# Three modulation pairs moved from the state loop into the transposed projections

## The chip, the cores and the metric

The kernel runs on one core of one Trainium2 chip. The metric is the device time of one execution in microseconds; the median of three runs of the kernel before is 743.1 us. The engines are PE (TensorE), DVE (VectorE), ACT (ScalarE), POOL (GpSimd) and SP (SyncE, which here only issues DMAs). Each works through its own list of instructions in order and waits on semaphores.

## What is computed

One step of a one-layer hybrid encoder, for 512 prompt rows and 32 sample rows of width 1024, in fp32. Cut to what matters here:

```
sh1, sc1, gt1, sh2, sc2, gt2 = split(silu(c) @ ada_w + ada_b, 6)      # c: one row for the prompt, one for the sample
h = x * (1 + sc1) + sh1
gq, gk, gv, gr, ga, sq, sk, sv = split(h @ w_in)                       # one combined projection
loga = log_sigmoid(ga @ a2_w + a2_b) / 16
o_gla, state = chunkwise gated linear attention of gq, gk, gv, loga    # 4 heads, chunks of 64 rows
o_swa = windowed attention of sq, sk, sv                               # 8 heads, 2 of keys, window 128
mix = concat(rms_norm(o_gla) * silu(gr), o_swa) @ w_o
x = layer_norm(2**0.25 * x + gt1 * mix)
h2 = x * (1 + sc2) + sh2
x = layer_norm(2**0.25 * x + gt2 * mixture_of_experts(h2))             # 32 experts, the top 2 of a group
```

## The kernel before

Every engine has a list written out by hand; nothing reorders it. The stages follow one another in the profile like this.

**Modulation.** The 6144 columns of `ada_w` are cut into 12 pairs of 512 columns. A pair is two loads of 1 MB (units `("ada", 2p)` and `("ada", 2p+1)`, the two halves of the contracted 1024 rows) and, on PE, `ada(p, bk)` (L879 to L897): 4 small matmuls for the bias and 32 matmuls with two stationary columns (prompt and sample) over 128 weight columns each. DVE copies the result out with `mod_evac` (four copies into `modst`, which raise `ada_ev`). Pairs 0 to 3 are sh1 and sc1 and come first, since `h` needs them. Pairs 4 and 5 are gt1, 6 and 7 sh2, 8 and 9 sc2, 10 and 11 gt2; these are the later pairs, needed only after the output projection.

**Transposed projections.** PE computes ten blocks with `proj_t(tb, ...)` (L927 to L943): ga, gq (two blocks), gk (two), sq0 (two: tb 5 and 6), sq1 (two: tb 7 and 8) and sk (tb 9, from the unit `kv`). Each fp32 product is done as three passes over a high and a low part of both factors. For that ACT copies each 1 MB weight unit into a rounded high part (`high_unit(q)`, raises `iw_h`) and DVE subtracts it to leave the low part (`low_unit(q)`, raises `iw_l`); PE waits for `iw_l`. ACT also copies every finished block out of PSUM (`evac_t(tb)`, raises `t_ev`), and `proj_t(tb)` waits for the copy of block tb-2. The order on ACT is fixed (L695 to L707): ..., `evac_t(6)`, `high_unit(4)` (the unit kv), three exponentials of 128x1088 for the gates, `evac_t(7)`, `evac_t(8)`, `high_unit(5)` (the unit gv0), `evac_t(9)`.

**Row projections and window attention.** `proj_kv` makes sv, sk by rows in banks 3 and 4, then the wide projections gv and gr (units gv0, gv1, gr0, gr1) are woven into the window attention.

**State loop** (L1085 to L1109). For each of five row tiles: PE transposes the decayed keys into bank 0 (L1090), ACT copies them out (L765), PE multiplies them with the values (L1102, banks 6 and 7), DVE updates the carried state (L1539, four small operations, raises `u_ev`), and the next product waits for that. In the first three turns PE also computes pairs 4, 5 and 6 (`ADA_STATE`), with the copy-out on DVE ahead of that turn's state update.

**GLA output** computes scores and outputs, with pairs 7, 8 and 9 between (`ADA_GLA`), then the output projection, routing, and 36 expert turns that stream 3 MB of weights each.

**Weight loads.** SP issues them in the order of the list `units`: the eight ada units of pairs 0 to 3, the nine projection units gq, gk, sq0, sq1, kv, gv0, gv1, gr0, gr1, the twelve ada units of pairs 4 to 9, four units of `w_o`. They go into a ring of five 1 MB slots. Ahead of each load SP waits until the slot's former unit has been used:

```
if former(n) is not None:
    sp.wait_ge(*freed(former(n)))
```

A wait on SP holds up every load behind it. The slot of kv was last held by ada unit 7, so in this kernel its load is asked for once the fourth pair is done, ahead of the projections. After `gr1` the ada units of pair 4 wait for the units gv0 and gv1 to be used, the next three for the end of all row projections.

**Tiles.** `areaC` is a scratch area; its first 2560 columns hold the values `gv`, which DVE writes only during the window attention. `modst` is part of `modrt`, whose whole width also holds the attention scores of every other row tile (`Ssc[1]`).

Of the kernel before, what the change touches and what calls it, by code (L numbers as in the profile page):

```python
# [5 lines left out]
def hymba_stream_step(nc, x_prompt, x_sample, c_prompt, c_sample, state_gla, cache_swa_k, cache_swa_v,  # L6
# [71 lines left out]
    for u in range(NA1, NA2):  # L78
        units.append(("ada", u))
# [14 lines left out]
    with ctx:  # L94
# [101 lines left out]
        gt2_tiles = [[ring[:, NR - 1, :], gt2w], [ring[:, FREE, :], gt2w]]  # L196
        gt2st = areaC[0:98, 8 * D:8 * D + UC]
# [79 lines left out]
        h_high, h_low, ga_high = sem("h_high_parts"), sem("h_low_parts"), sem("ga_high")  # L277
        s_gtw = [sem("gt2_weights0"), sem("gt2_weights1")]
# [90 lines left out]
        ADA_STATE = {0: NPAIR1, 1: NPAIR1 + 1, 2: NPAIR1 + 2}  # L369
# [19 lines left out]
        FIRST = [(1, 2), (0, 2), (0, 0), (0, 1), (1, 0), (2, 0), (1, 1), (2, 1), (2, 2)]  # L389
# [4 lines left out]
        def _(sp):  # L394
# [3 lines left out]
            for n, (kind, u) in enumerate(units):  # L398
# [15 lines left out]
                if former(n) is not None:  # L414
                    sp.wait_ge(*freed(former(n)))
                for g, src in unit_src(kind, u):
                    if kind == "wo":
                        v = slot_view(n, 2)
                        dst = v if g is None else v[g * HD:(g + 1) * HD, :, :]
                    elif kind in ("ada", "gv0", "gv1", "gr0", "gr1"):  # L420
                        dst = slot_view(n, KD // 2)
                    elif kind in ("sq0", "sq1"):
                        dst = slot_view(n, KD)[:, :, g * HD:(g + 1) * HD]
                    else:
                        dst = slot_view(n, KD)
                    sp.dma_start(dst, src).then_inc(full[place(n)], 16)
# [58 lines left out]
        def _(pool):  # L485
# [44 lines left out]

            pool.wait_ge(tok_ev, NT)
# [24 lines left out]
            def store_mod(c, n, staged):  # L556
                for t in range(4):
                    dst = mod_d[:, c * D:(c + n) * D].rearrange("b (p t c) -> b p t c", t=4, c=P)[:, :, t, :]
                    pool.dma_start(dst, staged[32 * t:32 * t + 2, :].rearrange("b (p c) -> b p c", c=P)).then_inc(s_mod, 16)

            pool.wait_ge(ada_ev, NPAIR1 + 2)
            store_mod(2, 1, modst[:, 4 * P:6 * P])
# [3 lines left out]
            store_mod(3, 2, modst[:, 6 * P:10 * P])  # L566
# [12 lines left out]
            store_mod(5, 1, gt2st)  # L579
# [288 lines left out]
        def _(pe):  # L868
# [10 lines left out]
            def ada(p, bk):  # L879
                if p < NPAIR2:  # L880
# [10 lines left out]
                for k in range(KD):  # L891
                    if k == KD // 2 and p < NPAIR2:
                        wait_unit(ns[1])
# [76 lines left out]
            for q in (2, 3):  # L970
                pe.wait_ge(iw_l, q + 1)
                for b in range(2):
                    proj_t(tb, unit_parts(q), slice(b * P, (b + 1) * P)).then_inc(pe_t, 1)
                    tb += 1
            pe.wait_ge(iw_l, 5)
# [3 lines left out]
            pe.transpose(bank[1][:, 0:WIN], kc[:, :], ident[:, :]).then_inc(pe_t, 1)  # L979


            def proj_kv(m):
# [3 lines left out]
                if m >= 2:  # L986
                    pe.wait_ge(tok_ev, m - 1)
# [97 lines left out]
            for j in range(NT + 1):  # L1085
                if j < NT:
                    r = ROWS[j]
                    pe.wait_ge(kd_ev, j) if j >= 1 else pe.wait_ge(z_ev, 10)
# [17 lines left out]
                if j in ADA_STATE:  # L1106
                    p = ADA_STATE[j]
                    pe.wait_ge(tok_ev, len(TOK)) if j < 2 else pe.wait_ge(ada_ev, p - 1)
                    ada(p, 3 + p % 2)  # L1109
# [16 lines left out]
            def gla_out(j):  # L1126
# [5 lines left out]
                else:  # L1132
                    pe.wait_ge(ada_ev, NPAIR1 + 3)
# [219 lines left out]
        def _(dve):  # L1353
# [77 lines left out]
            low_unit(4)  # L1431

# [28 lines left out]

            low_unit(5)
            for m in range(NT):
# [9 lines left out]
            def scores(j, g):  # L1473
# [6 lines left out]
                for par in range(2):  # L1480
                    dve.wait_ge(pe_qk, 4 * j + 2 * g + par + 1)
                    h0 = 4 * par + 2 * g
# [43 lines left out]
            for j in range(NT):  # L1526
                if j in ADA_STATE:
                    mod_evac(ADA_STATE[j], 3 + ADA_STATE[j] % 2)
# [333 lines left out]
```

## Time and profile before

| | |
|---|---|
| median of 3 runs | 743.1 us (741.85 to 743.35) |
| the profiled execution | 743.77 us, of which 741.5 us from its first to its last instruction |
| busy in it | PE 617.3 us (83%), DVE 327.8 us, ACT 135.0 us, POOL 103.2 us |
| loads in the span | 181.03 MB, mean 244 GB/s |

All times of the trace are counted from the first instruction. The lead-in ends near 40 us, the transposed projections fill 40 to 114 us, the row projections and the window attention 114 to 225 us, the state loop 225 to 248 us, the GLA output 248 to 294 us, output projection and routing 294 to 407 us, the experts 408 to 700 us, and the last sums and norms the rest. Shares of busy time are averages over all of these.

### The profile page before, as it was taken

To read this page: it belongs to the slowest core of one execution; us is meant where nothing else is said; L and a number is where in the kernel's file an instruction comes from. 1 tells how busy PE (TensorE), PEld (TensorE's weight loads), DVE (VectorE), ACT (ScalarE), POOL (GpSimd) and SP (SyncE) were. 2 spreads that over 40 slices of the span, in tenths; PEclk is the share of its full clock that TensorE was granted. 3 is DMA by queue.
4 is the path that set the end of the run, shared out by engine and by line. 5 is a ranking of instruction groups with operands and counts; after the bars stand their busy time and mean duration, and the time that the engine had idled before them with its cause. 6 is when DMAs were issued, how large, how long until landed. Compare 5 with 4: busy or idle time off the path is not lost.

```text
span 741.5 us, 10794 instructions
## 1 busy us (share of the span) xinstructions
PE 617.3 (83%) x4458; PEld 392.8 (53%) x4458; DVE 327.8 (44%) x592; ACT 135.0 (18%) x356; POOL 103.2 (14%) x144
## 2 busy tenths in 40 slices
PE   3679999899998798999754999888888878878494
PEld 2459999676765564454443655444444444435241
DVE  2463361655524552375675245433333333343248
ACT  1442351334343053011120100000000000000100
POOL 3000000100001202000012233322222222222100
PEclk9979999999998587999955899988999999989797
DMA  8981330003009798501499599999999999996243
GB/s 301 369 220 58 66 114 2 14 1 114 1 3 383 257 384 213 197 29 42 170 364 356 196 408 408 408 405 407 406 408 408 408 400 398 402 399 267 77 187 117
DMA packets 75899, 181.03 MB, mean 244 GB/s; under 512 B 22164, under 2 KB 26108, under 8 KB 75844
## 3 DMA queue, kind: packets, MB, share of 16 engines
q1 hardware_dynamic: 65220, 163.39, 59.5%
q0 software_dynamic: 7936, 14.09, 5.5%
q10 hardware_dynamic: 2688, 2.77, 1.1%
q8 instruction: 40, 0.66, 0.4%
q14 instruction: 15, 0.12, 0.0%
HBM read 176.25 MB, written 14.45 MB: 257 GB/s over the span
## 4 chain that ended last, share of the span: by engine, by line
PE 48%; SPq 25%; DVE 11%; DMA 8%; issue 4%; ACT 3%; DVEq 0%; ACTq 0%; POOLq 0%
SPq L431 24%; PE bank L941 9%; PE bank L1175 7%; PE bank L1279 6%; PE bank L1008 6%; PE bank L1297 3%; DMA ring<-in_moe_w_up_dram 3%; DMA ring<-in_ada_w_dram 2%; PE bank L895 2%; PE bank L990 2%; DMA x_tok<-in_x_sample_dram 2%; PE bank L1138 1%; PE bank L1061 1%; PE bank L1142 1%; PE bank L1032 1%
## 5 line engine op out<-in xcount | busy, mean ns | idle before, releaser
L1279 PE MATMUL bank<-late_w,xT 128*64 128x256 f32 x672 | 88.5, 423 | 19.8 <-DMA late_w<-in_moe_w_up_dram 15.9
L1279 PEld LDWEIGHTS bank<-late_w,xT 128*64 128x64 f32 x672 | 55.1, 152 | 59.3 <-DMA late_w<-in_moe_w_up_dram 26.5
L1279 PE MATMUL bank<-ring,xT 128*64 128x256 f32 x480 | 65.6, 435 | 16.9 <-DMA ring<-in_moe_w_up_dram 15.1
L1759 DVE COPY xT<-bank 128x512 f32<-128x512 f32 x36 | 24.7, 692 | 124.1 <-PE bank L1265 123.7
L1279 PEld LDWEIGHTS bank<-ring,xT 128*64 128x64 f32 x480 | 39.6, 157 | 47.2 <-DMA ring<-in_moe_w_up_dram 23.9
L838 ACT ACTIVATE sgl<-bank 128x128 f32<-128x128 f32 x36 | 10.0, 278 | 250.0 <-PE bank L1279 250.0
L601 POOL DMA_INDIRECT expert_rows<-ye,dsti x36 | 36.6, 1016 | 125.1 <-DVE ye L1778 125.1
L594 POOL DMA_INDIRECT xg<-h_scratch,srci x38 | 38.9, 1025 | 105.7 <-PE bank L1265 94.1
L1775 DVE SCALAR_TENSOR_TENSOR S<-bank,modrt,S 128x512 f32<-128x512 f32 x36 | 27.0, 751 | 37.3 <-PE bank L1297 37.3
L1297 PE MATMUL bank<-late_w,hT 128*64 128x512 f32 x168 | 40.7, 604 | 1.2 <-issue 1.2
L1008 PE MATMUL bank<-ring_r,h_high 128*128 128x512 f32 (+1 forms) x140 | 38.4, 415 | 0.0
L895 PE MATMUL bank<-ring,csT 128*2 128x128 f32 x704 | 30.9, 342 | 4.5 <-DMA ring<-in_ada_w_dram 4.5
L941 PE MATMUL bank<-h_high,ring_r 128*128 128x272 f32 (+2 forms) x224 | 32.4, 293 | 0.0
L941 PEld LDWEIGHTS bank<-h_high,ring_r 128*128 128x128 f32 x224 | 29.9, 188 | 0.8
L1297 PE MATMUL bank<-ring,hT 128*64 128x512 f32 x120 | 29.1, 604 | 1.2 <-issue 1.2
L1008 PEld LDWEIGHTS bank<-ring_r,h_high 128*128 128x128 f32 (+1 forms) x140 | 23.8, 178 | 8.9 <-issue 1.8
L1175 PE MATMUL bank<-ring,areaA 128*128 128x512 f32 x64 | 28.5, 598 | 0.0
L1175 PE MATMUL bank<-ring,areaB 128*128 128x512 f32 x64 | 28.1, 592 | 0.0
L895 PEld LDWEIGHTS bank<-ring,csT 128*2 128x2 f32 x704 | 20.1, 102 | 14.4 <-DMA ring<-in_ada_w_dram 5.3
L1265 PE MATMUL bank<-ident,xg 128*128 128x128 f32 x144 | 23.8, 291 | 4.6 <-DMA xg<-h_scratch,srci 4.6
L1776 DVE SCALAR_TENSOR_TENSOR ye<-bank,modrt,S 128x512 f32<-128x512 f32 x36 | 26.7, 742 | 0.0
L1778 DVE TENSOR_TENSOR ye<-ye,S 128x512 f32<-128x512 f32 x36 | 24.9, 692 | 1.2
(309 smaller groups left out, 883.3 us busy)
## 6 DMA issues: line engine op xcount, KB each, us to landing
ring<-in_ada_w_dram SPq DMA_DIRECT2D x22, 1024.0 KB, 10.3
late_w<-in_moe_w_gate_dram SPq DMA_DIRECT2D x21, 1024.0 KB, 16.5
late_w<-in_moe_w_up_dram SPq DMA_DIRECT2D x21, 1024.0 KB, 20.1
late_w<-in_moe_w_down_dram SPq DMA_DIRECT2D x21, 1024.0 KB, 19.9
ring<-in_moe_w_down_dram SPq DMA_DIRECT2D x15, 1024.0 KB, 20.1
ring<-in_moe_w_gate_dram SPq DMA_DIRECT2D x15, 1024.0 KB, 16.4
ring<-in_moe_w_up_dram SPq DMA_DIRECT2D x15, 1024.0 KB, 20.2
ring<-in_w_in_dram SPq DMA_DIRECT2D x7, 1024.0 KB, 6.0
```

Source lines behind the costliest of these rows:

```text
L431: sp.dma_start(dst, expert_src(e, r)).then_inc(w_gu[k] if r < 2 else w_dn[k], 16)
L594: pool.indirect_dma_start(out=xg[:, a, :], out_offset=None, in_=h2_d[:, :], in_offset=bass.IndirectOffsetOnAxis(ap=srci[:, b:b + 1], axis= ...
L601: pool.indirect_dma_start(out=yb_d[:, :], out_offset=bass.IndirectOffsetOnAxis(ap=dsti[:, b:b + 1], axis=0), in_=ye[:, a, :], in_offset=No ...
L895: mm = pe.matmul(bank[bk][32 * t:32 * t + 2, 0:P], cs3[:, :, k], w[2 * k // KD][:, k % (KD // 2), t * P:(t + 1) * P], start=False, stop=(k ...
L941: mm = pe.matmul(bank[bk + tb % 2][0:m, 0:ts.stop - ts.start], w[pw][:, k, cs], hHL[ph][:, k, ts], start=(ph + pw == 0 and k == 0), stop=( ...
L1008: mm = pe.matmul(bank[3 + m % 2][0:r, :], hHL[ph][:, half * KD // 2 + k, tok(j)], w[pw][:, k, :], start=(half == 0 and ph + pw == 0 and k ...
L1175: mm = pe.matmul(bank[1 + 2 * (j % 2) + half][0:r, :], mix, v[:, kk, half * 512:(half + 1) * 512], start=(k == 0), stop=(k == KD - 1))
L1279: mm = pe.matmul(bank[2 + a][f * C:(f + 1) * C, 0:2 * P], x, w[:, kk, f, :, :], start=(kk == 0), stop=(kk == KD - 1))
L1297: mm = pe.matmul(bank[5 + a][c * C:(c + 1) * C, :], hT2[:, a, f * C:(f + 1) * C], w[:, f, c * HALF:(c + 1) * HALF], start=(f == 0), stop=( ...
L1775: dve.scalar_tensor_tensor(yt[:, :], y, wsl[:, 0, b:b + 1], gtw[:, 0, :], ALU.mult, ALU.mult).then_inc(y_part, 1)
L1776: dve.scalar_tensor_tensor(ye[:, a, :], y, wsl[:, 1, b:b + 1], gtw[:, 1, :], ALU.mult, ALU.mult).then_inc(y_part, 1)
L1778: dve.tensor_tensor(ye[:, a, :], ye[:, a, :], yt[:, :], ALU.add).then_inc(y_ev2, 1)
```

## The change

Pairs 4, 5 and 6 are taken out of the ring and out of the state loop. Their weights go into two 1 MB tiles that lie over the space of the values (`early_tiles`, columns 0 to 4095 of `areaC`). SP issues them from within its list: pair 4's two loads ahead of the unit sq0, pair 5's ahead of the unit kv, pair 6's ahead of the unit gv1. The tiles are used three times, so ahead of pair 5's loads SP waits until pair 4 is done, and ahead of pair 6's until pair 5 is done. PE computes pair 4 after the blocks of sq0 (bank 3), pair 5 after those of sq1 (bank 4), pair 6 after the transpose of the cached keys (bank 0). DVE copies pair 4 out behind `low_unit(4)`, pair 5 behind the products for the GLA operands, pair 6 behind `low_unit(5)`. `proj_kv` waits for the copies of pairs 4 and 5 (its banks), the state loop for that of pair 6. POOL stores these three pairs to DRAM at once, ahead of its other stores, and DVE waits for that store before it writes scores over `modst`. With six units fewer in the ring the slots of the later units move by places, and the order of the first nine expert loads is rewritten for that.

```diff
-    for u in range(NA1, NA2):
+    NEARLY = 3
+    for u in range(NA1 + 2 * NEARLY, NA2):
         units.append(("ada", u))
...
+        early_tiles = [areaC[:, b * KD * UC:(b + 1) * KD * UC] for b in range(2)]
...
-        ADA_STATE = {0: NPAIR1, 1: NPAIR1 + 1, 2: NPAIR1 + 2}
+        EARLY_AT = {number[("sq0", 0)]: 0, number[("kv", 0)]: 1, number[("gv1", 0)]: 2}
...
-        FIRST = [(1, 2), (0, 2), (0, 0), (0, 1), (1, 0), (2, 0), (1, 1), (2, 1), (2, 2)]
+        FIRST = [(1, 2), (1, 1), (0, 2), (0, 0), (0, 1), (2, 0), (1, 0), (2, 1), (2, 2)]
...
                 if former(n) is not None:
                     sp.wait_ge(*freed(former(n)))
+                if n in EARLY_AT:
+                    i = EARLY_AT[n]
+                    if i >= 1:
+                        sp.wait_ge(pe_mod, NPAIR1 + i)
+                    for b in range(2):
+                        sp.dma_start(early_tiles[b].rearrange("p (k n) -> p k n", k=KD // 2),
+                                     ada_half(NA1 + 2 * i + b)).then_inc(s_early[i], 16)
                 for g, src in unit_src(kind, u):
...
+            pool.wait_ge(ada_ev, NPAIR1 + NEARLY)
+            store_mod(NPAIR1, NPAIR1 + NEARLY)
             pool.wait_ge(tok_ev, NT)
...
                 for b in range(2):
                     proj_t(tb, unit_parts(q), slice(b * P, (b + 1) * P)).then_inc(pe_t, 1)
                     tb += 1
+                ada(NPAIR1 + q - 2, 3 + q - 2)
             pe.wait_ge(iw_l, 5)
             proj_t(tb, unit_parts(4), slice(0, 2 * HD)).then_inc(pe_t, 1)
...
+            pe.wait_ge(z_ev, 10)
+            ada(NPAIR1 + 2, 0)
...
-                if m >= 2:
-                    pe.wait_ge(tok_ev, m - 1)
+                pe.wait_ge(*((ada_ev, NPAIR1 + m + 1) if m < 2 else (tok_ev, m - 1)))
...
-                if j in ADA_STATE:
-                    p = ADA_STATE[j]
-                    pe.wait_ge(tok_ev, len(TOK)) if j < 2 else pe.wait_ge(ada_ev, p - 1)
-                    ada(p, 3 + p % 2)
...
             low_unit(4)
+            mod_evac(NPAIR1, 3)
...
+            mod_evac(NPAIR1 + 1, 4)
             low_unit(5)
+            mod_evac(NPAIR1 + 2, 0)
...
+                    if j == 1 and g == 0:
+                        dve.wait_ge(s_mod, 64)
```

The order of instructions shows what this does at three places. On SP, from the loads of sq1 to those of gr0 and gr1, before (128x8x64 is a quarter of sq1, 128x8x256 is kv, 128x4x512 are gv0, gv1 and, last, gr0 and gr1; `rw` and `rb` are router weights; `mod_units_done` counts finished pairs):

```order
L426 DMA ring<-in_w_in_dram 128x8x64 [waits mod_units_done]
L426 DMA ring<-in_w_in_dram 128x8x64 x3
L426 DMA ring<-in_w_in_dram 128x8x256 [waits mod_units_done]
L426 DMA ring<-in_w_in_dram 128x4x512 [waits proj_T_done] x2
L409 DMA rw<-in_router_g_w_dram 128x8x4
L411 DMA rw<-in_router_e_w_dram 128x8x8 x4
```

and on the same stretch of SP now:

```order
L436 DMA ring<-in_w_in_dram 128x8x64 [waits mod_units_done]
L436 DMA ring<-in_w_in_dram 128x8x64 x3
L424 DMA areaC<-in_ada_w_dram 128x4x512 [waits mod_units_done]
L424 DMA areaC<-in_ada_w_dram 128x4x512
L436 DMA ring<-in_w_in_dram 128x8x256
L436 DMA ring<-in_w_in_dram 128x4x512 [waits proj_T_done]
L424 DMA areaC<-in_ada_w_dram 128x4x512 [waits mod_units_done,proj_T_done]
L424 DMA areaC<-in_ada_w_dram 128x4x512
L436 DMA ring<-in_w_in_dram 128x4x512
```

The load of kv now stands behind two loads of pair 5 and their wait for pair 4, and gv1 behind those of pair 6 and their wait for pair 5.

On PE, the end of the transposed projections before (bank 5 is the last block of sq1, 128x512 begins the block of sk, `kc` are the cached keys, bank 3 the first row projection):

```order
L941 MATMUL bank5<-h_low,S_r 128x272 x8
L941 MATMUL bank2<-h_high,ring_r 128x512 [waits proj_T_evacuated,proj_weights_low]
L941 MATMUL bank2<-h_high,ring_r 128x512 x15
L941 MATMUL bank2<-h_low,ring_r 128x512 x8
L941 MATMUL bank6<-h_high,ring_r 128x32 x16
L941 MATMUL bank6<-h_low,ring_r 128x32 x8
L979 MATMUL bank1<-ident,kc 128x128 [waits proj_T_evacuated,cache_loaded]
L990 MATMUL bank3<-ring_r,h_high 128x256 [waits proj_weights_low]
```

and there now (the rows with `adab` and `csT` are a pair):

```order
L956 MATMUL bank5<-h_low,S_r 128x272 x8
L904 MATMUL bank4<-adab,ident 2x128 [waits mod_weights_early1]
L904 MATMUL bank4<-adab,ident 2x128 x3
L910 MATMUL bank4<-areaC,csT 2x128 x32
L956 MATMUL bank2<-h_high,ring_r 128x512 [waits proj_T_evacuated,proj_weights_low]
L956 MATMUL bank2<-h_high,ring_r 128x512 x15
L956 MATMUL bank2<-h_low,ring_r 128x512 x8
L995 MATMUL bank1<-ident,kc 128x128 [waits proj_T_evacuated,cache_loaded]
L904 MATMUL bank0<-adab,ident 2x128 [waits mod_weights_early2,gate_evacuated]
L910 MATMUL bank0<-areaC,csT 2x128 x32
L1007 MATMUL bank3<-ring_r,h_high 128x256 [waits mod_evacuated,proj_weights_low]
```

Pairs 5 and 6 stand on either side of the block of sk; pair 4 stands in the same way ahead of the first block of sq1.

On PE, the start of the state loop before (`ident,areaB` are the key transposes, `areaC 64x128` the products for the state):

```order
L1090 MATMUL bank0<-ident,areaB 128x128 [waits gate_evacuated,mixT_swa,gla_operands_ready]
L889 MATMUL bank3<-adab,ident 2x128 [waits ring_full3,proj_tok_evacuated]
L895 MATMUL bank3<-ring,csT 2x128 x16
L895 MATMUL bank3<-ring,csT 2x128 [waits ring_full4]
L1090 MATMUL bank0<-ident,areaB 128x128 [waits kd_evacuated]
L1102 MATMUL bank6<-areaC 64x128 [waits proj_tok_evacuated,kd_evacuated]
L1102 MATMUL bank7<-areaC 64x128 x4
L889 MATMUL bank4<-adab,ident 2x128 [waits ring_full2,proj_tok_evacuated]
```

and there now:

```order
L1107 MATMUL bank0<-ident,areaB 128x128 [waits mod_evacuated,mixT_swa,gla_operands_ready]
L1107 MATMUL bank0<-ident,areaB 128x128 [waits kd_evacuated]
L1119 MATMUL bank6<-areaC 64x128 [waits proj_tok_evacuated,kd_evacuated]
L1119 MATMUL bank7<-areaC 64x128 x4
L1119 MATMUL bank6<-areaC 64x128 [waits state_updated,proj_tok_evacuated,kd_evacuated]
```

The loop holds only transposes and state products, and no wait for a ring slot.

## Rows read from the trace of the kernel before

**Rows 1.** The page's loads over the span, in 40 slices of 18.5 us.
```profile
GB/s 301 369 220 58 66 114 2 14 1 114 1 3 383 257 384 213 197 29 42 170 364 356 196 408 408 408 405 407 406 408 408 408 400 398 402 399 267 77 187 117
```

**Rows 2.** Busy time by stretch; the first line names the columns.
```profile
core 0: us, PE busy (x) PEld busy (x) DVE busy (x) ACT busy (x) POOL busy (x), PEclk, DMA share, GB/s
...
94.00:106.00 12.00, 12.00 (x97) 11.97 (x96) 7.21 (x9) 7.43 (x10) 0.00 (x0) 1.00 0.28 89
...
135.30:141.00 5.70, 5.63 (x22) 4.28 (x24) 1.11 (x5) 0.00 (x0) 0.00 (x0) 0.70 0.00 0
...
237.90:247.70 9.80, 5.45 (x76) 3.33 (x76) 6.69 (x17) 1.27 (x3) 0.00 (x0) 0.56 1.05 387
```

**Rows 3.** PE by time (start, length): sq1's first block, sk, row projections begin.
```profile
93.76 1.16 PE L941 MATMUL bank<-h_high,S_r 128*128 128x272 f32 x8
...
105.78 3.85 PE L941 MATMUL bank<-h_high,ring_r 128*128 128x512 f32 x16
...
114.02 2.14 PE L990 MATMUL bank<-ring_r,h_high 128*128 128x256 f32 x16
```

**Rows 4.** PE by time: pairs 4, 5 and 6 in the state loop.
```profile
225.91 3.34 PE L895 MATMUL bank<-ring,csT 128*2 128x128 f32 x64
...
230.15 0.40 PE L889 MATMUL bank<-adab,ident 24*2 24x128 f32 x8
...
232.34 0.44 PE L1090 MATMUL bank<-ident,areaB 128*128 128x128 f32 x2
...
237.94 1.06 PE L895 MATMUL bank<-ring,csT 128*2 128x128 f32 x32 [2.09 <-DMA ring<-in_ada_w_dram]
```

**Rows 5.** All engines by time: the chain of the state loop.
```profile
226.78 0.37 ACT L765 ACTIVATE areaC<-bank 128x256 f32<-128x256 f32 x1
...
241.08 1.50 DVE L1539 SCALAR_TENSOR_TENSOR S<-S,gend,bank 128x128 f32<-128x128 f32 x4
...
242.73 1.15 PE L1102 MATMUL bank<-areaC 64*64 64x128 f32 x16 [1.59 <-DVE S L1539]
244.02 1.50 DVE L1539 SCALAR_TENSOR_TENSOR S<-S,gend,bank 128x128 f32<-128x128 f32 x4 [0.71 <-PE bank L1102]
...
247.76 3.06 PE L1122 MATMUL bank<-areaB 64*128 64x128 f32 x16 [0.98 <-DVE S L1539]
```

**Rows 6.** ACT by time: the high part of kv, the exponentials, `evac_t(7)`.
```profile
94.53 1.91 ACT L683 ACTIVATE ring_r<-ring 128x2048 fp32r<-128x2048 f32 x1
96.47 1.28 ACT L701 ACT_TABLE_LOAD   x1
...
101.06 0.39 ACT L666 ACTIVATE areaB<-bank 128x272 f32<-128x272 f32 x1
```

**Rows 7.** Loads of line 426 issued in three short stretches, with time to landing.
```profile
L426 SPq DMA_DIRECT2D ring<-in_ada_w_dram x2: 367/437/507, 173.5 to 173.9; - x2
DMA to landing us min/median/max: 5.1/6.8/8.5
...
L426 SPq DMA_DIRECT2D ring<-in_ada_w_dram x1: 367/367/367, 26.1 to 26.1; - x1
L426 SPq DMA_DIRECT2D ring<-in_w_in_dram x1: 507/507/507, 26.5 to 26.5; - x1
DMA to landing us min/median/max: 9.7/11.0/12.3
...
L426 SPq DMA_DIRECT2D ring<-in_ada_w_dram x2: 507/507/507, 221.4 to 221.9; - x2
DMA to landing us min/median/max: 7.5/9.9/12.4
```

**Rows 8.** PE by time after its first wait behind the row projections.
```profile
135.37 1.04 PE L1032 MATMUL bank<-skT,areaB 64*128 64x128 f32 x8 [3.28 <-DVE areaC L1483]
136.34 3.51 PE L1008 MATMUL bank<-ring_r,h_high 128*128 128x512 f32 x8
...
146.01 2.14 PE L1008 MATMUL bank<-ring_r,h_high 128*128 128x512 f32 x8
```

More of the change, by code:

```diff
@@ L277, in hymba_stream_step @@
         h_high, h_low, ga_high = sem("h_high_parts"), sem("h_low_parts"), sem("ga_high")
+        s_early = [sem(f"mod_weights_early{i}") for i in range(NEARLY)]
         s_gtw = [sem("gt2_weights0"), sem("gt2_weights1")]
@@ L528, in _, with store_mod @@
             link(pool.memset(ones_b[:, :], 1.0))
+            def store_mod(p0, p1, staged=None):
+                staged = modst[:, p0 * P:p1 * P] if staged is None else staged
+                for t in range(4):
+                    dst = mod_d[:, 4 * P * p0:4 * P * p1].rearrange("b (p t c) -> b p t c", t=4, c=P)[:, :, t, :]
+                    pool.dma_start(dst, staged[32 * t:32 * t + 2, :].rearrange("b (p c) -> b p c", c=P)).then_inc(s_mod, 16)
+            pool.wait_ge(ada_ev, NPAIR1 + NEARLY)
+            store_mod(NPAIR1, NPAIR1 + NEARLY)
             pool.wait_ge(tok_ev, NT)
@@ L554, in sample_rows @@
                 pool.dma_start(modS[a][0:LS, :], mod_d[1:2, c].to_broadcast([LS, D])).then_inc(s_mods, 16)
[L556 to L562, printed above, removed]
             pool.wait_ge(s_mod, 64)
@@ L565, in _ @@
             pool.wait_ge(ada_ev, NPAIR2)
-            store_mod(3, 2, modst[:, 6 * P:10 * P])
+            store_mod(NPAIR1 + NEARLY, NPAIR2)
             pool.wait_ge(s_mod, 128)
@@ L578, in _ @@
             pool.wait_ge(gt2_ev, NPAIR - NPAIR2)
-            store_mod(5, 1, gt2st)
+            store_mod(NPAIR2, NPAIR, gt2st)
             pool.wait_ge(pe_y, NT)
@@ L879, in ada @@
             def ada(p, bk):
-                if p < NPAIR2:
+                if NPAIR1 <= p < NPAIR1 + NEARLY:
+                    pe.wait_ge(s_early[p - NPAIR1], 32)
+                    w = [t.rearrange("p (k n) -> p k n", k=KD // 2) for t in early_tiles]
+                elif p < NPAIR2:
                     ns = [number[("ada", 2 * p + i)] for i in range(2)]
@@ L891, in ada @@
                 for k in range(KD):
-                    if k == KD // 2 and p < NPAIR2:
+                    if k == KD // 2 and (p < NPAIR1 or NPAIR1 + NEARLY <= p < NPAIR2):
                         wait_unit(ns[1])
@@ L1087, in _ @@
                     r = ROWS[j]
-                    pe.wait_ge(kd_ev, j) if j >= 1 else pe.wait_ge(z_ev, 10)
+                    pe.wait_ge(kd_ev, j) if j >= 1 else pe.wait_ge(ada_ev, NPAIR1 + NEARLY)
                     for half in range(2):
@@ L1132, in gla_out @@
                 else:
-                    pe.wait_ge(ada_ev, NPAIR1 + 3)
+                    pe.wait_ge(tok_ev, len(TOK))
                 for par in range(2):
@@ L1526, in _ @@
             for j in range(NT):
-                if j in ADA_STATE:
-                    mod_evac(ADA_STATE[j], 3 + ADA_STATE[j] % 2)
                 r = ROWS[j]
```

## The prediction

> **What bounds the kernel now.** Read first how a shift of the early stages reaches the end. The loads over the span [rows 1] run at 398 to 408 GB/s from the 24th slice on (from 426 us), which is the experts' weights; in the 23rd (408 to 426 us), where PE begins the first expert, they move only 196 GB/s, so by then the five expert buffers are full and SP waits for PE to free one. The start of the expert stream therefore follows PE, and whatever moves PE's arrival at 408 us moves the end by as much. Then read the two places that the change touches. In the projections PE never stops: from 94 to 106 us it is busy 12.00 of 12.00 us at the full clock [rows 2], and the blocks stand end to end (sq1 begins at 93.76, sk at 105.78, the row projections at 114.02) [rows 3]. Work put in there is paid in full. In the state loop PE is busy 5.45 of the last 9.8 us, at a mean granted clock of 0.56 [rows 2]; what ends last there is a chain of products on PE and state updates on DVE, and the three pairs stand in it.
>
> **Part 1: what leaves the state loop.** Pair 4 runs at 225.91 for 3.34 us, pair 5 from 230.15 to 232.34, pair 6 has its last half held by a load to 237.94 [rows 4]. The chain without them is built from its last turns: a state update begins at 241.08, the next at 244.02, so a turn costs 2.94 us, with the product of 1.15 us that belongs to the lower clock level [rows 5]. The first keys are copied out at 226.78 + 0.37 = 227.15; the second transposes (0.44 us at the full clock [rows 4], more at the lower) and the first product (1.15) follow, so the first update can begin at about 229.0, the third two turns later at 234.9. In the trace the third begins at 241.08. **Gain 6.2 us.** If the first two products still run at the full clock, each some 0.4 us shorter, it is up to 7; if ACT, which has a silu ahead of each copy, holds the first turns by a few tenths each, 5.5. The pairs' copies on DVE leave with them and are in these numbers.
>
> **Part 2: the same three pairs among the projections.** Pair 5, at the full clock, takes 230.15 to 232.34 [rows 4], 2.2 us. PE has no gap there, so three cost **6.6 us**. Parts 1 and 2 alone nearly cancel: the state loop loses little more than the pairs' own PE time.
>
> **Part 3: the load of kv behind a wait.** This decides. Before, kv was loaded ahead of the projections. Now SP may not ask for it until pair 4 is done, and pair 4 stands behind sq0: 93.9 + 2.2 = 96.1 us. Then SP issues two loads of pair 5, then kv, some 0.5 us apart. Two 1 MB loads alone land 5.1 us after the first issue and 0.4 + 8.5 = 8.9 us after it [rows 7]. For a third with rows of 1 KB like kv's: one of this kind, issued 0.4 us behind an ada load, landed at 26.5 + 12.3 = 38.8 us, 3.0 us after the one ahead of it at 26.1 + 9.7 = 35.8 [rows 7]. So kv lands at 96.2 + 8.9 + 3.0 = 108.1 us. Bounds: three ada loads issued from 221.0 took until 221.9 + 12.4 = 234.3, 13.3 us, with other loads beside them [rows 7], which gives 109.5; at the stream's 408 GB/s [rows 1] 3 MB take 7.7 us, and with the 2.5 us that the single load of 5.1 us has over its 2.6 us at that rate, 106.4.
>
> Who waits: on ACT the high part of kv (1.91 us) waits for the load, and queued behind it are a table load, three exponentials and the copy of block 7. From the start of the high part to the end of that copy the trace has 94.53 to 101.45, 6.9 us [rows 6]. PE's block of sk needs that copy. Before, it was done at 101.45 for a start at 105.78, 4.3 us of cover. Now it is done at 108.1 + 6.9 + 0.1 = 115.1, while PE is through sq1 and pair 5 at 105.75 + 4.4 = 110.15. **Wait 4.95 us**, from 3.3 (kv at 106.4) to 6.3 (at 109.5). DVE's low part of kv (2.3 us after the high part, 112.4) lies inside it.
>
> The Trainium skill's page "DMA: Bandwidth & Descriptors" (Anatomy of one DMA) fits a transfer as 2.0 us plus its bytes at 436 GB/s, for another issue path than SP's. By that estimate 3 MB land 9.2 us after 96.2, the wait is 2.3 us, and the median would come out at 745.9 (without the next term), still slower. The pair of loads in rows 7 took 8.9 us where the fit has 6.8, so the rows are taken.
>
> **Part 4: the clock after that wait.** Where PE waited 3.28 us, the next eight wide matmuls took 3.51 us and the granted clock of that stretch was 0.70; the same eight take 2.14 us at 146.01 [rows 2, 8]. Nearest row to a wait of 5 us, so **1.5 us**; from 0 (a shorter wait) to 3 (twice the loss, as the wait is longer).
>
> The page "TensorE: Matmul & The Clock Gate" of the Trainium skill (Why this matters for your kernels) advises against idle gaps between bursts, as matmuls after one run at the slower of two clocks; that speaks against the change twice, for the new wait and for a state loop without filling. Rows 2 agree for the loop: 0.56 already with the pairs in it, so the products are taken at the lower level throughout.
>
> **Edits costed at nothing, with their cover.** Pair 4's loads stand ahead of sq0 and sq1, which are asked for in the lead-in, and delay them by some 6 to 9 us [rows 7]; sq1 is wanted at 93.76 and sq0 two blocks, 12 us, earlier [rows 3]. gv0 lands some 3.5 us after kv, at 112; its high part on ACT comes at 116. Pair 6's loads are asked for at 110.2 and land at 119; PE wants them at about 125. gv1 follows 3 to 4 us later, the router weights and gr0, gr1 after that; all are split only behind the row projections, at about 142. DVE's GLA products slip as the exponentials do, by 13.6 us; behind them stand pair 5's copy, gv0's low part and pair 6's copy. The second row projection wants the first of these at about 130, and if DVE were late there PE would stand still by as much. POOL's early store has until the second tile's scores, some 25 us after pair 6. Pairs 7 to 9 and `w_o` wait for the same events as before, so their loads keep their places. The new order of the first expert loads moves one of nine from just before the end of the output projection to just behind it; the first expert comes long after.
>
> **The sum**, on the profiled execution of 743.77 us: 743.77 - 6.2 + 6.6 + 4.95 + 1.5 = 750.6. The median of the runs is 0.7 us below that execution, so 749.9 is forecast for the median: **6.8 us, 0.9%, slower.** What a measurement here can tell from no change is about 0.2%, 1.5 us. The ends: everything low, -7 + 6.6 + 3.3 + 0 = +2.9, 746.0; everything high, -5.5 + 6.8 + 6.3 + 3 = +10.6, 753.7.
>
> **Rivals.**
> A, not slower: kv is not late. PE waits for nothing if kv has landed by 110.15 - 6.95 = 103.2 us, 7.0 us after SP asks for the first of the three loads. For it: 3 MB at the full 408 GB/s are 7.7 us, not far off. Against: every row of two or three loads in a row is slower than that, and a single one takes 5.1. Its time is 743.1 - 6.2 + 6.6 = 743.5, no change; with the gain at its upper bound 742.7.
> B, faster: the three pairs cost PE less between the blocks than alone, since their 32 matmuls use two stationary columns and PE might overlap them with the next block, and kv is in time. If half of 6.6 us went, 740.2. Against: in the lead-in and in the state loop they stand end to end with other work and take their 2 us.
> C, slower by more: after the wait PE stays at the lower level through the whole block of sk. The block is 114.02 - 105.78 = 8.2 us [rows 3]; at the ratio of rows 8, 3.51 to 2.14, it takes 5.3 us more instead of 1.5: 753.7. Against: the stretch with the loss in rows 2 is 5.7 us at 0.70, so the loss ended inside it.
> D, the change saves less than it says: the state loop is held by ACT's silu and table load, and only 3 us go. 753.1. For it: the first copy ends at 227.15, 2 us into the stage. Against: ACT is busy 1.27 us of the last 9.8 [rows 2].
>
> **How the numbers follow.** Forecast (kv late by 3.3 to 6.3 us, clock loss up to 3) 0.72; A 0.09; B 0.04; C 0.07; D 0.08. The range begins halfway between A and the forecast's low end, at 744.8, for a wait that is partly covered, and ends at 753.7, which takes in the high end, C and D; A, B and the outer mixtures, some 0.15, stay out. Slower by over 0.2%: forecast, C and D, 0.87, less 0.03 for a wait that is mostly covered, 0.84; within 0.2%: those and most of A, 0.10; faster: B and the rest of A, 0.06.
>
> **What would show it.** In the profile after: kv issued near 97 and landed near 108; ACT idle for some 13 us ahead of the high part of kv, released by that load; PE idle for about 5 us ahead of the block of sk, released by ACT, and its first matmuls longer than 3.85 us for sixteen; the row projections beginning near 128 and the window attention's first scores near 142 (+13.1); a state loop of some 16.5 us instead of 22.7. It is wrong if kv lands before 104, if ACT's copy of block 7 is not what PE waits for, or if the later stages don't keep the shift.

## The result and the profile after

The changed kernel takes 749.24 us in the median (746.33 to 754.78, 8 runs) against 743.9 us (741.85 to 748.3, 8 runs) for the kernel before: a ratio of 1.0076, 95% interval 1.0051 to 1.0101, or 5.3 us slower by the medians and 5.7 by the ratio. Single runs of either kernel scatter by several us. Below, a difference of an experiment from the kernel before is its ratio times the time of the kernel before, run beside it; differences of the medians lie up to 1.0 us from these. Other differences are between the stages of two profiles. Three of the first twelve runs of e6 (747.2 to 748.3 us) were in a slower state and are left out of its ratio. The profiled execution took 748.88 us, its span 746.5 us.

All engines of the changed kernel by time, from pair 4 to pair 6 (start, length, engine, line, operation, tiles, count, and in brackets the idle time ahead with what ended it; `SPq` is SP's DMA queue). Here and in the fences below, rows in between are left out:

```profile
96.08 1.93 PE L910 MATMUL bank<-areaC,csT 128*2 128x128 f32 x64
98.13 0.92 SPq L424 DMA_DIRECT2D areaC<-in_ada_w_dram  x2
99.09 3.37 SPq L436 DMA_DIRECT2D ring<-in_w_in_dram  x2
108.93 1.92 ACT L695 ACTIVATE ring_r<-ring 128x2048 fp32r<-128x2048 f32 x1 [12.38 <-DMA ring<-in_w_in_dram]
110.50 1.93 PE L910 MATMUL bank<-areaC,csT 128*2 128x128 f32 x64
115.45 0.39 ACT L678 ACTIVATE areaB<-bank 128x272 f32<-128x272 f32 x1
115.97 3.92 PE L956 MATMUL bank<-h_high,ring_r 128*128 128x512 f32 x16 [3.54 <-ACT areaB L678]
125.04 3.23 PE L910 MATMUL bank<-areaC,csT 128*2 128x128 f32 x64
```

Pair 4 releases SP at 98.1. It asks for the two loads of pair 5 and only then for kv, which lands at 108.9, 10.8 us after the first of the three was asked for. ACT has stood idle for 12.38 us; its high part, the exponentials and the copy of block 7 run until 115.45 + 0.39 = 115.84, and PE, done with pair 5 at 112.4, waits 3.54 us for that copy. Before, PE went from sq1 into sk without a gap [rows 3].

Busy time by stretch, same kernel (length, then PE, PEld, DVE, ACT, POOL busy, the granted clock as a share of 2.4 GHz, DMA share, GB/s): the wait, the block of sk, pair 6.

```profile
112.40:116.00 3.60, 0.06 (x5) 0.06 (x1) 2.46 (x10) 3.60 (x6) 0.00 (x0) 1.00 0.66 189
115.90:124.40 8.50, 8.43 (x49) 7.34 (x49) 8.26 (x10) 2.33 (x4) 0.00 (x0) 1.00 1.01 308
124.40:128.20 3.80, 3.80 (x73) 2.17 (x72) 1.56 (x1) 0.85 (x3) 0.00 (x0) 0.56 0.52 38
```

The block behind the wait runs at the full clock (3.92 us for its first sixteen matmuls, 3.85 before [rows 3]). The loss comes one block later, in pair 6 (granted clock 0.56), with PE busy all the time.

All engines, then PE alone: the state loop, the first expert, the last sums.

```profile
240.02 0.41 PE L1107 MATMUL bank<-ident,areaB 128*128 128x128 f32 x2 [0.41 <-issue]
...
242.19 0.69 PE L1107 MATMUL bank<-ident,areaB 128*128 128x128 f32 x2 [1.75 <-ACT areaC L777]
...
244.47 1.50 DVE L1555 SCALAR_TENSOR_TENSOR S<-S,gend,bank 128x128 f32<-128x128 f32 x4 [1.89 <-PE bank L1119]
...
247.41 1.50 DVE L1555 SCALAR_TENSOR_TENSOR S<-S,gend,bank 128x128 f32<-128x128 f32 x4 [0.71 <-PE bank L1119]
...
415.45 4.11 PE L1292 MATMUL bank<-ring,xT 128*64 128x256 f32 x18 [0.94 <-DVE xT L1775]
...
708.21 7.00 PE L1346 MATMUL bank<-x_tok,ident 128*128 128x512 f32 x12 [8.76 <-issue]
```

The two kernels stage by stage, each length from the first row of one stage to the first row of the next:

| stage | before | after | second profile of after |
|---|---|---|---|
| end of sq0's blocks to first scores | 34.6 | 46.8 (+12.2) | 49.3 (+14.7) |
| first scores to state loop | 96.7 | 97.4 (+0.8) | 96.6 (-0.1) |
| state loop | 22.7 | 17.0 (-5.7) | 17.0 (-5.7) |
| GLA output | 46.6 | 44.4 (-2.3) | 43.7 (-2.9) |

The first expert begins at 415.45 (before 408.62) and the last sums at 708.21 (before 702.81), so the shift is kept, as the prediction assumed, less 1.4 us among the last experts, where one turn's 32 matmuls take 3.67 us instead of 5.36. Ahead of these stages, pair 4 begins at 95.8, 2.0 us after the place it takes in the kernel before, since the ga block and the gates' product with the block behind it, which the change doesn't touch, ran 0.9 and 1.5 us longer, at a lower granted clock (0.72 instead of 0.88 in the ga block, 0.74 instead of 1.00 behind it). In the second profile pair 4 begins 0.8 us ahead of that place, so this isn't put down to the change.

### The profile page after: what moved, and what is told of

Same layout as the page of the kernel before. It is cut to its first block, busy times and chain, and to the rows that moved or that the text cites. A ratio compares the mean times of both kernels' runs of the same rounds, so it can differ in the third digit from the quotient of the medians.

```text
span 746.5 us, 10798 instructions
## 1 busy us (share of the span) xinstructions
PE 616.7 (83%) x4458; PEld 391.3 (52%) x4458; DVE 327.5 (44%) x592; ACT 134.7 (18%) x356; POOL 103.2 (14%) x144
## 4 chain that ended last, share of the span: by engine, by line
PE 47%; SPq 25%; DVE 11%; DMA 8%; ACT 5%; issue 4%; DVEq 0%; ACTq 0%; POOLq 0%
SPq L441 24%; PE bank L1188 7%; PE bank L956 7%; PE bank L1292 6%; PE bank L1025 6%; PE bank L1310 3%; DMA ring<-in_moe_w_up_dram 3%; PE bank L910 2%; PE bank L1007 2%; DMA x_tok<-in_x_sample_dram 2%; DMA ring<-in_ada_w_dram 1%; DMA ring<-in_w_in_dram 1%; PE bank L1151 1%; PE bank L1078 1%; PE bank L1049 1%
## 5 line engine op out<-in xcount | busy, mean ns | idle before, releaser
L1292 PE MATMUL bank<-late_w,xT 128*64 128x256 f32 x672 | 86.8, 417 | 21.4 <-DMA late_w<-in_moe_w_up_dram 17.4
L1292 PEld LDWEIGHTS bank<-ring,xT 128*64 128x64 f32 x480 | 38.7, 155 | 46.8 <-DMA ring<-in_moe_w_up_dram 23.8
L1418 DVE TENSOR_TENSOR ring_r<-ring,ring_r 128x2048 fp32r<-128x2048 f32 x6 | 13.6, 2286 | 28.3 <-ACT ring_r L695 28.3
L545 POOL DMA_DIRECT2D mod_scratch<-modrt x8 | 4.8, 609 | 148.3 <-DVE modrt L1393 148.3
```

The costliest lines, as they stand in the source:

```text
L1292: mm = pe.matmul(bank[2 + a][f * C:(f + 1) * C, 0:2 * P], x, w[:, kk, f, :, :], start=(kk == 0), stop=(kk == KD - 1))
```

## The experiments

**e1: kv ahead of every early load.** Pair 5's loads now stand ahead of gv1 and pair 6's ahead of gr0, still behind their waits for the pair before.

```
-EARLY_AT = {number[("sq0", 0)]: 0, number[("kv", 0)]: 1, number[("gv1", 0)]: 2}
+EARLY_AT = {number[("sq0", 0)]: 0, number[("gv1", 0)]: 1, number[("gr0", 0)]: 2}
```

> The changed kernel with pair 5's two loads put ahead of gv1 instead of kv, and pair 6's ahead of gr0 instead of gv1; nothing else differs. Theory (the wait for kv and the clock loss behind it cost 3.5 + 1.6 us of the change's +5.3): PE goes from pair 5 into the block of sk without a wait, pair 6 runs at the full clock, and the time comes to +0.2 us against the kernel before, that is the pairs' 6.6 on PE less the state loop's 5.7 and some noise: between -1 and +1.5. Rival 1 (the place of kv's load does not matter, the pairs or the state loop cost it): stays at +5. Rival 2 (gv1 or gr0, now late, take kv's place as what PE waits for): +2 to +4, with a new wait ahead of the window attention.

Measured 747.77 us against 743.39 before, ratio 1.0045 (1.0019 to 1.0070): +3.3 us (4.4 between the medians), more than expected. PE by time:

```profile
109.43 3.95 PE L956 MATMUL bank<-h_high,ring_r 128*128 128x512 f32 x16
118.22 0.40 PE L904 MATMUL bank<-adab,ident 24*2 24x128 f32 x8 [0.22 <-DMA areaC<-in_ada_w_dram]
118.56 3.54 PE L910 MATMUL bank<-areaC,csT 128*2 128x128 f32 x64
```

The wait ahead of sk is gone, yet pair 6 is at the lower level again (granted clock 0.56 from 118.2 to 122.1). So that loss comes without the wait too. Pair 6's own load, which waits for pair 5, now lands just as PE wants it: PE waits 0.22 us for it here, and 2.46 us in the second profile (r1 below).

**e2: e1 with the three pairs computed twice**, to price a pair on a PE without slack.

```
+for turn in range(2 if NPAIR1 <= p < NPAIR1 + NEARLY else 1):
     ...                                        # the pair's 36 matmuls
```

> The same with pairs 4, 5 and 6 each computed twice on PE, from the same weights into the same bank. Theory (PE has no slack there, a pair costs its 2.2 us): 6.6 us more than with the pairs once, +6.8 against the kernel before. Rival (the pairs ride on slack in the projections): no more than 2 us above the same kernel with the pairs once.

Measured 752.86 us, 1.0131 (1.0100 to 1.0161): 6.4 us above e1 by the ratios, 5.1 by the medians. PE by time, pair 4 twice:

```profile
94.13 1.93 PE L911 MATMUL bank<-areaC,csT 128*2 128x128 f32 x64
96.31 1.93 PE L911 MATMUL bank<-areaC,csT 128*2 128x128 f32 x64
```

The second copy begins 2.18 us after the first, and so it is with pairs 5 and 6. Nothing hides a pair there; rival B falls.

**e3: copy of block 7 ahead of the high part of kv on ACT**, the rest as in the changed kernel.

```
 evac_t(6)
+evac_t(7)
 high_unit(4)
 ...
-evac_t(7)
 evac_t(8)
```

> The changed kernel with kv's load left late, but on ACT the copy of block 7 moved ahead of the high part of kv. Theory (what PE waits for is that copy, queued on ACT behind kv's high part and three exponentials): the block of sk then begins when kv's low part is done, 2.3 us after its high part, at about 113.2 instead of 116.0; 2.7 us less than the changed kernel, +2.6 against the kernel before; +1 if the shorter wait keeps the clock up in pair 6. Rival (PE waits for the low part anyhow): +5.3.

Measured 746.3 us, 1.0037 (1.0013 to 1.0060): +2.75 us, as expected. PE by time:

```profile
110.59 3.94 PE L956 MATMUL bank<-h_high,ring_r 128*128 128x512 f32 x16 [0.85 <-DVE ring_r L1418]
119.93 3.60 PE L910 MATMUL bank<-areaC,csT 128*2 128x128 f32 x64
123.46 3.06 PE L1007 MATMUL bank<-ring_r,h_high 128*128 128x256 f32 x16
```

The block of sk begins after a wait of 0.85 us instead of 3.54, now for DVE's low part of kv. That the queue on ACT turns the late load into the wait is shown. The lower level stays all the same: pair 6 and the first row projection lose 2.8 us together, more than in the first profile of the changed kernel.

**e4: the kernel before with kv late, alone.** SP waits for seven finished blocks and loads 2 MB to spare ahead of kv; the pairs stay in the state loop. PE waits for the spare loads ahead of the row projections, by when they have long landed.

```
+if n == number[("kv", 0)]:
+    sp.wait_ge(pe_t, 7)
+    ...                                        # two 1 MB loads into a spare place
 ...
+pe.wait_ge(s_spare, 32)
 for m in range(NT):
     proj_kv(m)
```

> The kernel before with one thing added: SP waits for the blocks of sq0 ahead of kv's load and issues two spare 1 MB loads ahead of it, into space that is free then; the pairs stay in the state loop. Theory: kv lands 10.8 us after the wait, at 104.8, block 7 is copied out at 111.8, and the block of sk begins there instead of at 105.8: +6.0, and up to +7.6 with the clock loss of 1.6 behind the wait. Rival (a late kv is taken up later, by the wait behind the row projections): under +2.

Measured 755.2 us, 1.0157 (1.0128 to 1.0185): +11.7 us, more than expected. SP, ACT and PE by time:

```profile
93.10 0.92 SPq L421 DMA_DIRECT2D areaC<-in_ada_w_dram  x2
104.85 1.91 ACT L689 ACTIVATE ring_r<-ring 128x2048 fp32r<-128x2048 f32 x1 [11.12 <-DMA ring<-in_w_in_dram]
111.89 5.45 PE L947 MATMUL bank<-h_high,ring_r 128*128 128x512 f32 x16 [6.86 <-ACT areaB L672]
121.73 3.50 PE L996 MATMUL bank<-ring_r,h_high 128*128 128x256 f32 x16
```

The block of sk begins 7.0 us after the landing, as the 6.9 us of ACT's queue [rows 6] have it, and here the block behind it is at the lower level (5.45 us for sixteen matmuls instead of 3.85) and so is the first row projection (3.50 instead of 2.14). From sq1 to the first scores it takes 10.1 us more: 6.9 of wait and 3.1 of clock. kv landed 11.75 us after the first of the three loads was asked for, where the changed kernel has 10.8; here gv0 and gv1 are asked for right behind kv.

**e5: e1 with pair 6 in the gap of 3.28 us in the window attention** [rows 8].

```
-pe.wait_ge(z_ev, 10); ada(NPAIR1 + 2, 0)      # behind sk
 ...
 fill(j, 0)
+if j == 0: ...; ada(NPAIR1 + 2, 0)             # ahead of the second scores
 ...
 qk(j, 1)
```

> The order of e1 (kv loaded ahead of all early weights), with pair 6 moved from behind the block of sk to the window attention: on PE between the first half of the first wide projection and the first tile's second scores, where the kernel before and the changed one stand idle for 3.28 us, waiting for DVE. Theory: pairs 4 and 5 cost 4.4 us on a PE without slack, pair 6 at full clock (2.2 us) lies inside the 3.28 us, the lower clock that e1 had around pair 6 (some 1.5 us) is gone from the end of the projections, and the state loop gives 5.7 us: -5.7 + 4.4 = -1.3 us against the kernel before, within 1.5 either way. Rival: the lower clock belongs to that stretch of time whatever stands in it and is found in the first row projections instead, +0.2 to +0.5 us; or the pair runs in the gap at the lower clock, 3.7 us, and is paid for by 0.4 us of it.

Measured 744.1 us, 1.0005 (0.9977 to 1.0033), no difference from before. PE by time:

```profile
112.56 3.95 PE L956 MATMUL bank<-h_high,ring_r 128*128 128x512 f32 x16
120.89 3.57 PE L1005 MATMUL bank<-ring_r,h_high 128*128 128x256 f32 x16
...
140.73 1.93 PE L910 MATMUL bank<-areaC,csT 128*2 128x128 f32 x64
143.76 1.04 PE L1047 MATMUL bank<-skT,areaB 64*128 64x128 f32 x8 [1.09 <-DVE areaC L1501]
144.72 2.12 PE L1023 MATMUL bank<-ring_r,h_high 128*128 128x512 f32 x8
```

Pair 6 is free in the gap (1.09 of the 3.28 us are left), and the eight wide matmuls behind the filled gap run at full clock, 2.12 us instead of the 3.51 of [rows 8]. But the lower level now falls on the first row projection, 3.57 instead of 2.14 us, as its rival has it: it doesn't need the light work of pair 6 there.

**e6: pairs 5 and 6 both in that gap**, pair 5's weights over the gates' raw values, so that no load waits for a pair just computed.

```
-early_tiles = [areaC[:, b * KD * UC:(b + 1) * KD * UC] for b in range(2)]
+early_tiles = [[areaC[:, c + b * KD * UC:c + (b + 1) * KD * UC] for b in range(2)] for c in (0, 5 * D, 0)]
...
+if j == 0: ...; for i in (1, 2): ada(NPAIR1 + i, 0, P * i)
```

> Pair 4 stands behind the blocks of sq0 as in the changed kernel, pairs 5 and 6 both in the gap of 3.28 us in the window attention. Pair 5's weights lie over the space of the gates' raw values (columns 5120 to 9215 of areaC), so that no load waits for a pair just computed, and kv is loaded first. DVE's first scores wait for pair 5. Theory: 2.2 us paid for pair 4, 4.4 - 3.3 = 1.1 us for the two others, 5.7 us gained in the state loop: -2.4 us against the kernel before; -3.8 if the 1.4 us that the wide matmuls lose behind that gap in the kernel before go too, as PE no longer stands idle there. Rival: light work pulls the clock down as an idle PE does, the two pairs take 3.6 us each or the loss behind them is kept: -0.9 us or slower.

Measured 739.22 us, 0.9931 (0.9899 to 0.9964): -5.1 us, beyond what was expected. The mean of all twelve runs is 741.45 us, only 2.6 below the 744.05 of the kernel before. It ran again:

> The kernel of e6 once more, as its profile was of a disturbed run: it came out at 0.9931 of the kernel before, -5.1 us, where -0.9 to -3.8 was expected. If that was scatter, this comes out near -2.4 us (0.9968); if the idle gap that is now filled gives back more clock than rows showed, it is again near -5 us, and the profile shows the attention stage shorter than the 96.7 us of the kernel before by 1.4 us or more.

This time 742.61 us, 0.9979 (0.9947 to 1.0012), -1.6 us, which can't be told from no change. The -5.1 us did not come again, and the second profile has nothing that could give it: its attention stage is 98.5 us, 1.8 longer than before, where a real -5.1 us was to show one shorter by 1.4 or more. All engines by time in that profile:

```profile
137.51 1.93 PE L912 MATMUL bank<-areaC,csT 128*2 128x128 f32 x64
...
139.37 0.72 PE L1051 MATMUL bank<-skT,areaB 64*128 64x128 f32 x8
...
147.68 1.29 DVE L1505 SCALAR_TENSOR_TENSOR modrt<-bank,biasH 128x512 f32<-128x512 f32 x2 [2.03 <-DMA mod_scratch<-modrt]
...
148.42 1.73 PE L1051 MATMUL bank<-skT,areaB 64*128 64x256 f32 x8 [1.26 <-DVE modrt L1505]
```

The second scores come 8.0 us after the first, 1.0 us more than in the kernel before, as reckoned. But POOL's store of the pairs is now the last thing ahead of the second tile's scores: DVE waits 2.03 us for it and PE 1.26 us for DVE. In the changed kernel that store was early enough, as the prediction costed it.

**e7: pair 6 directly behind pair 5, ahead of the block of sk**, kv first. Pair 5's weights have a place of their own, as in e6, and the loads of pairs 5 and 6 stand ahead of gv0 and gv1, one unit earlier than in e1.

```
-EARLY_AT = {number[("sq0", 0)]: 0, number[("kv", 0)]: 1, number[("gv1", 0)]: 2}
+EARLY_AT = {number[("sq0", 0)]: 0, number[("gv0", 0)]: 1, number[("gv1", 0)]: 2}
...
+pe.wait_ge(z_ev, 10)
+ada(NPAIR1 + 2, 0)
 pe.wait_ge(iw_l, 5)
 proj_t(tb, unit_parts(4), ...)                 # sk
```

> Pair 6 directly behind pair 5, ahead of the block of sk instead of behind it, with the weights of pair 5 in a place of their own so that no load waits for it; kv loaded first as in e1. Same work on PE as e1 in another order. Theory (the narrow matmuls at the end of the block of sk and the pair behind them together pull the clock down): pair 6 takes 2.2 us at the full clock and the run is 1.5 us faster than e1, +1.8 us against the kernel before. Rival (any two pairs close together do it): pair 6 or the block of sk shows the lower level, the run equals e1, +3.3 us, or is up to 2 us slower.

Measured 743.39 us, 1.0004 (0.9975 to 1.0034): as fast as before.

```profile
108.66 1.93 PE L912 MATMUL bank<-areaC,csT 128*2 128x128 f32 x64
110.85 1.93 PE L912 MATMUL bank<-areaC,csT 128*2 128x128 f32 x64
112.71 3.95 PE L958 MATMUL bank<-h_high,ring_r 128*128 128x512 f32 x16
121.04 2.14 PE L1009 MATMUL bank<-ring_r,h_high 128*128 128x256 f32 x16
135.39 0.72 PE L1051 MATMUL bank<-skT,areaB 64*128 64x128 f32 x8
```

No loss anywhere: 41.47 us from the end of sq0's blocks to the first scores, 6.86 more than before, which is three pairs at 2.29 us. Neither kv nor a pair's weights are late. As e7 moves loads as well as PE's work, it doesn't tell which of the two keeps the clock up; e2, with the loads in e1's places, has no loss either.

**e8: e1 without the 32 matmuls of each early pair.**

```
-for k in range(KD):
+for k in range(0 if NPAIR1 <= p < NPAIR1 + NEARLY else KD):
```

> As e1, but of pairs 4, 5 and 6 only the four bias matmuls and the copies are computed; the 32 matmuls of each with the weights are left out (the loads stay). This is the gain of the state loop with nothing paid for it but about 0.3 us a pair. Theory (5.7 us gained in the state loop, nothing late): -5.7 + 0.9 = -4.8 us against the kernel before, and 8 us faster than e1 (three pairs 5.7 us, the lower clock some 1.5). Rival D of the prediction (the state loop gives 3 us): -2.1 us. No lower clock is expected at the end of the projections.

The total, 725.53 us, doesn't answer the question: the modulation that is left out changes the routing, and only 32 expert turns run instead of 36. PE by time:

```profile
121.88 0.60 PE L904 MATMUL bank<-adab,ident 24*2 24x128 f32 x8 [3.32 <-DMA areaC<-in_ada_w_dram]
...
235.52 0.41 PE L1107 MATMUL bank<-ident,areaB 128*128 128x128 f32 x2 [0.41 <-issue]
...
252.53 3.06 PE L1135 MATMUL bank<-areaB 64*128 64x128 f32 x16 [0.98 <-DVE S L1555]
```

The state loop takes 17.0 us here as in the changed kernel. So its gain is the loop's alone. PE now comes early enough to wait 3.32 us for the weights of pair 6, and the first row projection behind that wait is at the lower level (3.78 us), which was not expected.

**r0, r1, r7: the changed kernel, e1 and e7 once more**, to see whether the place of the clock's loss belongs to the order of the instructions.

> The changed kernel once more, for a second profile. The first had pair 6 at the lower clock level (3.7 us from 124.5) and none in the block of sk behind the wait of 3.54 us. If the place of the loss follows from the order of the instructions, it is there again: 3.6 to 3.8 us for pair 6, 3.9 us for the first sixteen matmuls of the block of sk. If it differs from execution to execution, it is at another place or absent.

> The kernel of e1 once more, for a second profile. The first had pair 6 at the lower level (3.54 us for its 64 rows of matmul and weight load instead of 1.93). Order of instructions as the cause: 3.2 to 3.6 again. Chance of the execution: 1.93 here, or the loss in another place.

> The kernel of e7 once more, for a second profile. The first had no loss of clock from pair 4 to the first scores (first row projection 2.14 us, both pairs 1.93). Order as the cause: the same again. Chance: a loss of 1.0 to 1.6 us shows up somewhere between pair 5 and the first scores, most likely in the first row projection, where the kernels with pair 6 elsewhere had it.

One run each: 751.81, 754.28 and 741.37 us. In r7 every row from pair 4 to the first scores has the length of e7's, again no loss. In r1 pair 6 takes 3.60 us and the first row projection 3.08 (in e1 3.54 and 2.16), and pair 6's load is late:

```profile
125.01 0.60 PE L904 MATMUL bank<-adab,ident 24*2 24x128 f32 x8 [2.46 <-DMA areaC<-in_ada_w_dram]
```

Its two loads landed 10.9 us after the first was asked for, in e1 8.6. In r0, PE by time and one stretch:

```profile
113.23 6.39 PE L956 MATMUL bank<-h_high,ring_r 128*128 128x512 f32 x16 [3.59 <-ACT areaB L678]
124.50 2.79 PE L910 MATMUL bank<-areaC,csT 128*2 128x128 f32 x64
127.22 2.87 PE L1007 MATMUL bank<-ring_r,h_high 128*128 128x256 f32 x16
```

```profile
112.90:116.90 4.00, 3.67 (x9) 2.94 (x10) 3.90 (x5) 2.56 (x4) 0.00 (x0) 0.50 1.05 401
```

Behind nearly the same wait, 3.59 us, the first sixteen matmuls of sk now take 6.39 us at half clock. The kernel is the same; where the level falls is not.

## Why the prediction was right, point by point

**Part 1, the state loop, held.** Forecast 6.2 us, 5.5 to 7; measured 5.7. The turns came as the rows had it: updates 2.94 us apart (244.47 to 247.41; 2.94 in [rows 5]), products of 1.15 us. The first update came at 244.47 - 240.02 = 4.45 us into the loop; forecast was 229.0 - 225.03 = 4.0. That is the difference: the second transposes take 0.69 us at the lower level instead of the 0.44 assumed, and the hand-over from PE to DVE the rest. Rival D is out.

**Part 2 held.** 6.6 us forecast; e7 measures 6.86 for three pairs at the full clock, and in e2 each second copy takes 2.2 us more.

**Part 3 held in its mechanism; the forecast wait was 1.4 us too long.** Forecast 4.95 us, bounds 3.3 to 6.3; measured 3.54 and 3.59. The term that was mis-sized is the landing of the third load: 96.2 + 11.9 was forecast, and it took 10.8 us, which is 1.1 of the 1.4 us; from pair 4 to the end of pair 5 PE took 0.3 longer than reckoned. By the fit of the Trainium skill's page "DMA: Bandwidth & Descriptors" (Anatomy of one DMA) the estimate was 9.2 us, so the measured time lies between the fit and the rows; the median of 745.9 us that goes with this estimate adds up to 745.8. The third load cost 1.9 us over the 8.9 of a pair of loads [rows 7], not the 3.0 read from the lead-in, where others ran beside it; e4, with more loads behind, has 11.75 for the three. From the landing to the copy's end it took the 6.9 us of [rows 6]. e1 and e3 take the wait away by two ways. Their totals gain 2.3 and 2.9 us by the ratios, each plus or minus some 2.6, so e1's is not clear of nothing; that the wait goes is read from the rows (none ahead of sk in e1, 0.85 us in e3). e4 brings such a wait about alone, and its total is clear. Rival A is out.

**Part 4 met its size by luck.** It put 1.5 us, 0 to 3, behind the wait. In the first profile the loss was nil there and 1.5 us in pair 6 (3.7 us from 124.5 to 128.2, where e7's pairs take 2.2), a loss that e1 has without the wait; in the second it was 2.5 us behind the wait (6.39 against 3.92) and 1.5 more in pair 6 and the first row projection, 4.0 together, above the upper bound. The step that failed is carrying [rows 8] over to another place: where PE waits 3.3 us in the window attention, the eight wide matmuls behind take 3.03 to 3.78 us in all eleven profiles that have this wait, and 2.12 to 2.14 in the three where pairs fill it (e5, e6 twice); a wait of 3.54 us here is followed by the lower level only in one of two executions. The page "TensorE: Matmul & The Clock Gate" of the Trainium skill (Why this matters for your kernels) puts the loss behind idle gaps; the waits in the window attention, r0 and e4 (6.86 us) agree; the first profile, with no loss right behind 3.54 us, and e1, e5 and e6, with a loss on a PE that had not stood idle for more than 0.3 us, don't. Rival C, the whole block of sk at the lower level, comes half way in r0, with 2.5 of its 5.3 us.

**The covers held.** sq1, gv0, gv1 and the router weights came in time, the second row projection did not wait, and the changed kernel's early store delayed nothing. DVE's copies fitted in.

**The sum.** Forecast +6.85 us; the three touched stages give +12.2 + 0.8 - 5.7 = +7.3 in the first profile. What the prediction did not have is the GLA output, 2.3 us shorter with the same instructions. Most of it is pair 9, at the full clock (before, then after):

```profile
276.29 3.60 PE L895 MATMUL bank<-ring,csT 128*2 128x128 f32 x64
283.83 1.93 PE L910 MATMUL bank<-ring,csT 128*2 128x128 f32 x64
```

The stage takes 43.7 to 44.5 us in both profiles of the changed kernel, of e1 and of e7 and in those of e2, e3 and e5, but 46.4 to 46.9 in e4, e6 (twice) and e8, as in the kernel before (46.6). Why is not settled. In the first profile, +7.3 in the touched stages, +2.0 in the lead-in, -2.3 in the GLA output and -2.0 behind it make the +5.0 us of the span. So the forecast's causes are there, but that the total comes so near is in part luck. The median of 749.24 us lies 0.7 us from the forecast 749.9, which was counted from 743.1; in the eight runs beside it the kernel before took 743.9, so the difference is 5.3 us where 6.8 was forecast. The row projections began at 128.20, as forecast, only because the 2.0 us of the lead-in stand against a shorter wait.

**What stays open** is what decides the place of the clock's loss at the end of the projections. It was there in every profile of the changed kernel, e1, e3, e4, e5, e6 and e8 (1.5 to 4.0 us) and absent in those of the kernel before, e2 and e7. Neither the wait nor the light work of a pair marks the first group off from the second. e7 gives the same picture twice, which speaks for the order of instructions and loads; by which rule, and whether two profiles are enough, these runs don't show.

## What to carry to other kernels

A load that is moved behind a wait in an in-order queue delays all that is queued behind it: price it as the landing of the last load of the burst, then follow it through the engine that consumes it (here ACT's queue of 6.9 us) before asking who waits. Moving work from a waiting stage into a saturated one pays its full price there; the same work pays nothing in a gap that something else holds open, if its copies and stores have time behind it. Look then for the next load that the same wait holds up: with kv issued first, e1 no longer waits ahead of sk, but pair 6's load is now the late one, by 0.2 and 2.5 us in its two profiles, and its total is not clear of the changed kernel's. e7, with the weights in places that free those loads and the light work in another order, took back all that was lost (1.0004 of the kernel before), and no more: what the state loop gains the projections pay.

## What the runs showed of the hardware

The same program lost the clock at different places in two executions, once behind a wait of 3.59 us and once not behind one of 3.54 us: the first sixteen matmuls behind took 6.39 us in the one and 3.92 in the other. A single profile is no proof of where such a loss belongs. Nor does a total show it: the two profiled times are 3 us apart (748.88 and 751.81), but the second execution is 1.8 us ahead when the output projection begins (299.61 against 301.37) and loses 3.9 us among the experts. In the window attention the lower level did belong to a place: behind 3.3 us of waiting it came in eleven profiles of eleven, and with pairs in that gap in none of three.

Three loads of 1 MB in a row on SP's queue landed 10.8 us after the first was asked for (10.85 in r0, 11.75 in e4), where two take 8.9 [rows 7], or 8.6 and 10.9 in the two profiles of e1.
